# First weight chunk's halves issued on ScalarE's DMA queue, tile pairs and weight pieces prepared in turn

## What is computed

```
x = x + 0.5 * swiglu(rmsnorm(x, norm_ff1[i]), ff1_w_gate[i], ff1_w_up[i], ff1_w_down[i])
...
def rmsnorm(x, g):
    y = xf * lax.rsqrt(jnp.mean(xf * xf, axis=-1, keepdims=True) + EPS)
    return (y * g.astype(jnp.float32)).astype(x.dtype)
def swiglu(h, w_gate, w_up, w_down):
    return (jax.nn.silu(h @ w_gate) * (h @ w_up)) @ w_down
```

## Time and profile before

| | us |
|---|---|
| median of 3 runs (lowest, highest) | 1175.71 (1175.65, 1175.8) |
| profiled execution, its own time | 1175.59 |
| its span, first to last instruction | 1173.7 |
| PE busy | 1166.6 |
| PEld busy | 1142.9 |
| DVE busy | 820.7 |
| ACT busy | 609.7 |
| POOL busy | 117.1 |
| mean granted clock of PE | 0.998 of full speed |

### The profile page before, as it was taken

How to read it: one execution, slowest core, us unless ns; L and a number is a source line. 1 busy time by engine, 2 the same in 40 slices (tenths; PEclk the granted TensorE clock), 3 DMA queues, 4 the chain that set the end, 5 groups by cost and what they waited for, 6 DMA issues and landing times.

```text
span 1173.7 us, 24027 instructions
## 1 busy us (share of the span) xinstructions
PE 1166.6 (99%) x10518; PEld 1142.9 (97%) x10518; DVE 820.7 (70%) x936; ACT 609.7 (52%) x688; POOL 117.1 (10%) x130
## 2 busy tenths in 40 slices
PE   9999999999999999999999999999999999999998
PEld 9999999999999999999999999999899999999998
DVE  6866545697978766655786665458799787666556
ACT  6544445555745644444764443446466555444445
POOL 2000001011512000001110000100134020000011
PEclk9999999999999999999999999999999999999999
DMA  8655555545445555555556555554644456555551
GB/s 294 232 202 190 189 206 169 193 150 200 154 145 194 200 193 201 192 187 198 191 175 224 183 203 189 183 214 140 220 145 146 143 204 211 205 182 202 192 180 37
DMA packets 33528, 218.87 MB, mean 186 GB/s; under 512 B 5200, under 2 KB 6544, under 8 KB 7440
## 3 DMA queue, kind: packets, MB, share of 16 engines
q1 hardware_dynamic: 32992, 216.82, 53.3%
q10 hardware_dynamic: 432, 0.52, 0.1%
HBM read 216.15 MB, written 1.05 MB: 185 GB/s over the span
## 4 chain that ended last, share of the span: by engine, by line
PE 98%; DMA 1%; DVE 1%; ACT 0%; SPq 0%; issue 0%; DVEq 0%
PE psum L409 32%; PE psum L410 31%; PE psum L411 31%; PE psum L691 1%; PE psum L670 1%; DMA x_all<-in_x 1%; PE psum L543 0%; PE psum L604 0%; PE psum L654 0%; PE psum L725 0%; DVE gates L1801 0%; PE psum L736 0%; PE psum L639 0%; PE psum L759 0%; DVE hB_lo L1769 0%; PE psum L586 0%
## 5 line engine op out<-in xcount | busy, mean ns | idle before, releaser
L1309 DVE TENSOR_TENSOR w_lo<-raw,w_hi 128x2048 fp32r<-128x2048 f32 x200 | 457.9, 2292 | 218.2 <-ACT w_hi L905 218.0
L905 ACT ACTIVATE w_hi<-raw 128x2048 fp32r<-128x2048 f32 x201 | 385.2, 1916 | 352.3 <-PE psum L411 347.7
L409 PE MATMUL psum<-hA_hi,w_hi 128*128 128x256 f32 x1360 | 377.6, 278 | 0.0
L410 PE MATMUL psum<-hA_hi,w_lo 128*128 128x256 f32 x1360 | 375.7, 276 | 0.0
L411 PE MATMUL psum<-hA_lo,w_hi 128*128 128x256 f32 x1360 | 375.7, 276 | 0.0
L409 PEld LDWEIGHTS psum<-hA_hi,w_hi 128*128 128x128 f32 x1360 | 255.4, 188 | 2.7 <-issue 2.7
L410 PEld LDWEIGHTS psum<-hA_hi,w_lo 128*128 128x128 f32 x1360 | 255.4, 188 | 0.0
L411 PEld LDWEIGHTS psum<-hA_lo,w_hi 128*128 128x128 f32 x1360 | 255.3, 188 | 0.0
L409 PE MATMUL psum<-hB_hi,w_hi 128*128 128x256 f32 x832 | 229.9, 276 | 0.6 <-DVE w_lo L1777 0.6
L410 PE MATMUL psum<-hB_hi,w_lo 128*128 128x256 f32 x832 | 229.7, 276 | 0.0
L411 PE MATMUL psum<-hB_lo,w_hi 128*128 128x256 f32 x832 | 229.7, 276 | 0.0
(11 more groups left out here) (207 smaller groups left out, 1241.4 us busy)
## 6 DMA issues: line engine op xcount, KB each, us to landing
raw<-in_weights SPq DMA_DIRECT2D x203, 1024.0 KB, 4.9
raw<-in_weights SPq DMA_DIRECT2D x2, 512.0 KB, 6.3
x_all<-in_x SPq DMA_DIRECT2D x1, 520.0 KB, 3.6
x_all<-in_x SPq DMA_DIRECT2D x1, 512.0 KB, 6.3
relu<-in_p SPq DMA_DIRECT2D x2, 256.0 KB, 5.1
consts<-in_consts SPq DMA_DIRECT2D x1, 384.0 KB, 5.1
out<-gates ACTq DMA_DIRECT2D x2, 192.0 KB, 2.3
out<-gates SPq DMA_DIRECT2D x2, 192.0 KB, 2.3
```

The lines of the kernel that those rows point to most:

```text
L409: pe.matmul(o, lh, rh, start=start, stop=False)
L410: pe.matmul(o, ll, rh, start=False, stop=False)
L905: act.activation(w_hi[:, s, :], raw[:, s, :], ACT.Copy).then_inc(hi_ready[s], 1)
L1309: dve.tensor_tensor(w_lo[:, s, :], raw[:, s, :], w_hi[:, s, :].bitcast(F32), ALU.subtract).then_inc(lo_ready[s], 1)
```

## The change

The two loads of chunk 0's halves go from SP to ACT's own DMA queue, as ACT's first instructions; SP issues the halves of x one after the other and then chunks 1 and 2. ACT and DVE take a pair and a piece in turn, for each m, where they took two pairs and then two pieces for each half. Semaphores and PE's program are unchanged.

```diff
--- before.py
+++ after.py
@@ -380,8 +380,6 @@
             for i in range(2):
                 part = slice(*X_HALVES[i])
                 sp.dma_start(x_all[:, part], a["x"][:, part]).then_inc(x_landed[i], 16)
-                half = slice(1024 * i, 1024 * i + 1024)
-                sp.dma_start(raw[:, 0, half], a["weights"][0, :, half]).then_inc(landed[0] if i else half_landed, 16)
             chunk(0, 1)
             chunk(0, 2)
             sp.dma_start(ident, a["consts"][:, 0:P]).then_inc(const_landed, 16)
@@ -1183,17 +1181,18 @@
                 assert steps[0] == SCALAR_STEPS, steps
                 steps[0] = 0
 
+            for i in range(2):
+                half = slice(1024 * i, 1024 * i + 1024)
+                act.dma_start(raw[:, 0, half], a["weights"][0, :, half]).then_inc(landed[0] if i else half_landed, 16)
             act.wait_ge(half_ready, 1)
             act.activation(rsum[:, 0, :], half_neg[:, 0:2], ACT.Copy)
-            for i in range(2):
-                act.wait_ge(x_landed[i], 16)
-                for m in (2 * i, 2 * i + 1):
-                    for c in (2 * m, 2 * m + 1):
-                        ins = act.activation(hB[0][:, c, :], x[:, c, :], ACT.Copy, scale=first_gains[:, c:c + 1])
-                    ins.then_inc(h_hi_ready, 1)
-                act.wait_ge(landed[0] if i else half_landed, 16)
-                for m in (2 * i, 2 * i + 1):
-                    act.activation(w_hi[:, 0, piece(m)], raw[:, 0, piece(m)], ACT.Copy).then_inc(piece_hi if m < 3 else hi_ready[0], 1)
+            for m in range(4):
+                act.wait_ge(x_landed[m // 2], 16)
+                for c in (2 * m, 2 * m + 1):
+                    ins = act.activation(hB[0][:, c, :], x[:, c, :], ACT.Copy, scale=first_gains[:, c:c + 1])
+                ins.then_inc(h_hi_ready, 1)
+                act.wait_ge(landed[0] if m // 2 else half_landed, 16)
+                act.activation(w_hi[:, 0, piece(m)], raw[:, 0, piece(m)], ACT.Copy).then_inc(piece_hi if m < 3 else hi_ready[0], 1)
             squares(0, 0, 0)
             act.wait_ge(landed[1], 16)
             for i in range(4):
@@ -1761,21 +1760,19 @@
                 assert steps[0] == VECTOR_STEPS - last, steps
                 steps[0] = 0
 
-            for i in range(2):
-                dve.wait_ge(x_landed[i], 16)
-                for m in (2 * i, 2 * i + 1):
-                    dve.wait_ge(h_hi_ready, of_norm(0, 0, m + 1))
-                    for c in (2 * m, 2 * m + 1):
-                        ins = dve.scalar_tensor_tensor(out=hB[1][:, c, :], in0=x[:, c, :], scalar=first_gains[:, c:c + 1],
-                                                       in1=hB[0][:, c, :].bitcast(F32), op0=ALU.mult, op1=ALU.subtract)
-                    ins.then_inc(h_ready, 1)
-                for m in (2 * i, 2 * i + 1):
-                    if m < 3:
-                        dve.wait_ge(piece_hi, m + 1)
-                    else:
-                        dve.wait_ge(hi_ready[0], 1)
-                    dve.tensor_tensor(w_lo[:, 0, piece(m)], raw[:, 0, piece(m)], w_hi[:, 0, piece(m)].bitcast(F32), ALU.subtract
-                                      ).then_inc(piece_lo if m < 3 else lo_ready[0], 1)
+            for m in range(4):
+                dve.wait_ge(x_landed[m // 2], 16)
+                dve.wait_ge(h_hi_ready, of_norm(0, 0, m + 1))
+                for c in (2 * m, 2 * m + 1):
+                    ins = dve.scalar_tensor_tensor(out=hB[1][:, c, :], in0=x[:, c, :], scalar=first_gains[:, c:c + 1],
+                                                   in1=hB[0][:, c, :].bitcast(F32), op0=ALU.mult, op1=ALU.subtract)
+                ins.then_inc(h_ready, 1)
+                if m < 3:
+                    dve.wait_ge(piece_hi, m + 1)
+                else:
+                    dve.wait_ge(hi_ready[0], 1)
+                dve.tensor_tensor(w_lo[:, 0, piece(m)], raw[:, 0, piece(m)], w_hi[:, 0, piece(m)].bitcast(F32), ALU.subtract
+                                  ).then_inc(piece_lo if m < 3 else lo_ready[0], 1)
             for i in range(4):
                 if i < 3:
                     dve.wait_ge(next_hi, i + 1)
```

## The result

Before 1175.8 us, after 1179.64 us (medians of seven runs each; 1175.65 to 1176.04 and 1179.0 to 1180.43). Ratio 1.0034, 95% interval 1.0025 to 1.0043: **slower by 3.8 us**, a third of a per cent. The forecast was 1176.2, within 1175.2 to 1177.3, and no change beyond 0.2%; all of it was wrong.

What follows compares the result with a forecast made beforehand. The chain of squares, not PE, was taken to bind at L463. Earlier issues counted 0, later x landing and turned order +0.5 us for the chain, giving 1176.2 us, range 1175.2 to 1177.3, no change beyond 0.2%.

Steps and rivals of the forecast that it cites:

- What bounds: At L463, the chain of squares, not PE, sets the time at 25.2 us, by about 0.2 us.
- Chunks 1 and 2 about 0.9 us earlier ... an earlier issue only lengthens a queue: 0: SP's issues: chunks 1 and 2 leave about 0.9 us earlier behind still busy engines, worth 0.
- Even sharing with a head start: First landings: queues share engines evenly, SP 0.3 us (0.10 MB) ahead; x half 0 at 6.2, weight half 0 at 6.9.
- 9.2 + 0.2: Landing of weight half 1: 9.2 us as before plus 0.2, just in time for its want at 9.8.
- The turned order costs only what the landings make of it: ACT's first chunk: one pair (0.80 us) falls behind the weights; +0.5 us with late x, 0.0 with landings as before.
- The term of POOL's additions: Top of the range: 0.5 us allowed for POOL's additions, which took 0.74 to 2.33 us beside DVE.
- The dip fills: Rival, 4.25 to 6.25 us: a second queue lifts 223 GB/s towards 431, -0.4 us, time 1175.3; chance 0.2.
- The clock: Rival: a longer gap before PE's first product halves its clock, up to 5.5 us more, 1181.7; chance 0.03.

Runs made afterwards that it cites:

- experiment 2: Kernel before with only the two weight halves issued by ACT, old order of pairs and pieces; 1178.63 us, ratio 1.0028.
- experiment 4: Changed kernel with chunks 1 and 2 issued by ACT behind its halves, leaving SP x and the small constants; 1178.25 us, in two groups.
- experiment 5: Changed kernel with ACT's two issues ahead of its eight semaphore increments, leaving at about 0.7 us; 1178.38 us, ratio 1.0022.
- experiment 8: experiment 1's kernel with DVE made to wait for POOL's first addition before its first piece of chunk 1; 1176.21 us, one group.
- experiment 1: Changed kernel with the two issues back on SP, so only the turned order of pairs and pieces remains; 1177.14 us, ratio 1.0009, two groups.
- 11: Changed kernel with chunks 1 and 2 as two loads each (4 KB rows), plus DVE's wait for POOL's first addition; 1178.13 us.
- 12: As 11, but chunks 1 and 2 in four loads of 2 KB rows each; 1177.87 us.
- 5 to 10: Besides those listed singly: four kernels with the first square moved into ACT's wait for weight half 0, halves on SP; 1175.54, 1177.03, 1175.98 and 1176.3 us.
- 3: Changed kernel with chunks 1 and 2 issued on SP as two loads each, rows of 4 KB instead of 8 KB; 1179.07 us.

## Why the prediction was wrong

- *What bounds*: right. L463 and the chain of squares set the time at 25.2 us, before and after; ACT's arrival at chunk 1 (+3.8) and L461 (+4.0) went together, while PE's own lag at the third quarter was 3.2. The margin is small: in experiment 2, where ACT was 0.8 us sooner at chunk 1, L461 had no wait.
- *"Chunks 1 and 2 about 0.9 us earlier ... an earlier issue only lengthens a queue: 0"*: **the step that failed.** It holds for one queue. With two, what stands on SP's queue behind x runs beside what stands on ACT's, packet for packet, and here it had 8 KB to ACT's 4 KB. From 5 to 8 us chunk 1 took some 0.6 MB of 1.21, more than the halves' 0.45. I had shared the engines between x and the weights' halves only, and so had the halves at 6.9 and "9.2 + 0.2" where ACT started on them at 9.38 and 13.05. With chunks 1 and 2 behind the halves (experiment 4) ACT started on half 0 at 7.67 and reached chunk 1 at 12.69 instead of 15.43: 2.7 of its 3.8 us of delay are this term. The other 1.0 is there in experiment 4 too, where ACT's first packets were as late and the constants ran beside the halves; no run parts these two.
- *"Even sharing with a head start"*: wrong in both numbers. x half 0 was hardly touched (4.6, not 6.2) and the weights were 9.36, not 6.9. A start of ACT 0.62 us behind SP gave SP not 0.1 MB but nearly all of x (in the changed kernel 0.91 MB of its 1.06 MB had moved at 4.9, before ACT's first packet). Only with equal starts (experiment 5) did they share from near the beginning.
- *The turned order costs only what the landings make of it*: half right. With landings as before it costs nothing where ACT reaches chunk 1 (experiment 8: 0.01 us). The term of POOL's additions, put at 0 to 0.5, was too small: the turned order costs 0.4 us with a gap for POOL (experiment 8) and 1.4 in the median without one (experiment 1, whose second square waited 1.48). In the trace of the changed kernel POOL got in between two of DVE's pieces (first addition 0.98 us, the piece behind it 1.13 instead of 0.68, second square 0.2 later than without it), so there the order adds by its place behind weight half 1: piece, pair, piece instead of two pieces, the 0.8 us between experiment 2's arrival and the changed kernel's.
- *The rivals*: none named this. "The dip fills" came true in the rate (408 GB/s from 4.25 to 6.25 for 223) and was worth nothing: of the 0.82 MB in these 2 us SP's queue had 0.57, the rest of x and the beginning of chunk 1, and the wanted halves had 0.25. The clock stayed at 1.00 through a gap of 2.90 us ahead of the first product.
- *The sum* of the parts, 2.9 for the queue (experiment 2) and 0.8 for the order behind it, is 3.7 of the measured 3.8; by the medians of these runs the second part is 1.0.

Left open: what holds ACT's first packets off until x is nearly through when they are issued 0.6 us late. That the engines first finish what they already hold of SP's queue fits experiments 4 and 5, and nothing here looks into the engines; the traces of 11 and 12 show how sharp it is, with ACT's issue 0.53 and 0.58 us behind SP's and its first packets at 4.3 and 4.5, after 0.65 and 0.75 MB of SP's. Nor did any run explain the low rate from 4.25 to 6.25 before. It was 219 to 236 GB/s in every trace in which x and the halves were under way together from the start (before, 1 and 5 to 10) and 367 to 408 in the others, where x came first and alone. Open too is why one run falls in the upper and another in the lower group.

## What to carry to other kernels

In these runs a second DMA queue didn't put a transfer first; it set it beside *everything* behind on the first queue, in the ratio of packet sizes. So before moving an urgent load ask what the emptied queue will issue in its place. The loads arrived in the order of use only where one queue issued them in that order. When an engine is made to run without gaps, look for the neighbour that lived in the gap: here a wait put back on VectorE won 0.9 us.

## What the runs showed of the chip that was not expected

- Packets of two busy queues alternate one for one, with sizes from 512 B to 8 KB: 65 to 62 with 8 KB beside 4 KB (6 to 8 us), 134 to 128 with 4 KB, 148 to 147 with mostly 2 KB beside 4 KB (both 5 to 8), 67 to 65 with mostly 512 B beside 4 KB (experiment 4, 6 to 7). The Trainium skill, DMA: Bandwidth & Descriptors, "Queues, rings and completion order", has round-robin by packets of some 9 to 17 descriptors; the turn by packets agrees, the size doesn't: with turns of a whole half (128 rows over 16 engines, 8 each), half 0 would have been in after one turn, not at 9.36 with some 0.6 MB of chunk 1 beside it by 8 us. This last is argued from the landings, not seen in a row.
- Smaller packets on one of two busy queues went with a lower sum from 5 to 8 us: 1.21 and 1.17 MB beside 8 KB rows (changed kernel, experiment 2), 0.99 and 1.04 beside 4 KB, 0.91 beside 2 KB. It is not the row size by itself: alone on the engines, the same rows made 0.44, 0.43 and 0.41 MB in one us (experiments 5, 3 and 12, from 10 or 11 us on). Why is open.
- 0.62 us between two queues' first issues made 3 us between their first packets (from before 1.9 to 4.9 us).
- GpSimd's addition of 0.74 us alone takes 2.3 beside VectorE's pieces of 0.68 us run back to back, and which of the two gets in first can change from run to run: 1.1 us between the groups of experiment 1.
